# Last expert rows with wide products and separate cross terms, splits two rows ahead, and two early rows placed before the turned picks

## What is computed

```python
q = rmsnorm(h) @ w_q                        # 8 heads
s = q_half @ sub_keys                       # 128 scores for each half of each head
top16 of each half, top16 of their sums     # 16 picks per head and token, weights by softmax
out = sum over picked experts e of  weight[t, e] * gelu(x[t] . u[e]) * v[e]
h = h + out;  return rmsnorm(h, final_norm_g)
```

## Time and profile before

| | |
|---|---|
| median of 3 runs | 1586.64 us (1583.40, 1586.64, 1588.95) |
| profiled execution | 1584.84 us, its span 1583.0 us |
| PE busy | 96% of the span |
| DVE, ACT, POOL busy | 74%, 54%, 22% |
| share of the last chain | PE 82%, DVE 13% |

### The profile page before, as it was taken

How to read it: one execution, slowest core, us unless ns; L and a number is a source line. 1 busy time by engine, 2 the same in 40 slices (tenths; PEclk the granted TensorE clock), 3 DMA queues, 4 the chain that set the end, 5 groups by cost and what they waited for, 6 DMA issues and landing times.

```text
span 1583.0 us, 32051 instructions
## 1 busy us (share of the span) xinstructions
PE 1526.1 (96%) x10720; PEld 1379.4 (87%) x10720; DVE 1178.0 (74%) x2312; ACT 851.2 (54%) x1573; POOL 354.2 (22%) x265
## 2 busy tenths in 40 slices
PE   9899998999999899899999899999999999999997
PEld 7788987999887786698999899988888899999996
DVE  5778676798848678455499778789999777777776
ACT  5564454666548654565455465554444555444455
POOL 3234332011100331222068765630000000000000
PEclk9889999999999999999999999999999999999999
DMA  8323244555565720254656555467777656655654
GB/s 287 119 94 120 81 139 154 153 186 184 187 187 173 253 76 1 80 187 147 194 161 217 183 176 156 152 199 240 242 240 241 210 187 186 185 185 185 187 185 158
DMA packets 89289, 272.22 MB, mean 172 GB/s; under 512 B 9984, under 2 KB 27520, under 8 KB 88832
## 3 DMA queue, kind: packets, MB, share of 16 engines
q1 hardware_dynamic: 65520, 238.06, 47.1%
q10 hardware_dynamic: 23696, 33.17, 6.6%
HBM read 259.13 MB, written 12.06 MB: 171 GB/s over the span
## 4 chain that ended last, share of the span: by engine, by line
PE 82%; DVE 13%; ACT 2%; issue 2%; DMA 1%; POOL 0%; DVEq 0%; ACTq 0%; SPq 0%
PE ps_chunk L508 22%; PE ps_misc L2966 22%; PE ps_chunk L514 11%; PE ps_misc L300 6%; PE ps_chunk L1931 4%; PE ps_chunk L501 3%; PE ps_chunk L520 3%; PE ps_misc L2901 3%; PE ps_chunk L300 2%; PE ps_chunk L524 2%; PE ps_chunk L529 1%; PE ps_misc L1010 1%; DVE mixers_arena L2680 1%; DVE mixers_arena L2679 1%; DVE mixers_arena L2676 1%
## 5 line engine op out<-in xcount | busy, mean ns | idle before, releaser
L425 ACT ACTIVATE w_hi<-raw 128x512 fp32r<-128x512 f32 (+2 forms) x898 | 546.6, 627 | 489.1 <-PE ps_chunk L514 193.7
L432 DVE TENSOR_TENSOR w_lo<-raw,w_hi 128x512 fp32r<-128x512 f32 x663 | 488.6, 755 | 247.1 <-ACT w_hi L425 238.0
L508 PE MATMUL ps_chunk<-x_hi,w_hi 128*128 128x256 f32 x1792 | 459.0, 288 | 2.0 <-ACT w_hi L425 1.6
L508 PE MATMUL ps_chunk<-x_lo,w_hi 128*128 128x256 f32 x1792 | 452.3, 285 | 0.0
L432 POOL TENSOR_TENSOR w_lo<-raw,w_hi 128x512 fp32r<-128x512 f32 (+2 forms) x237 | 311.3, 1329 | 518.8 <-ACT w_hi L425 454.8
L508 PEld LDWEIGHTS ps_chunk<-x_hi,w_hi 128*128 128x128 f32 x1792 | 345.8, 193 | 6.2 <-ACT w_hi L425 2.2
L508 PEld LDWEIGHTS ps_chunk<-x_lo,w_hi 128*128 128x128 f32 x1792 | 346.6, 193 | 2.9 <-issue 0.5
L514 PE MATMUL ps_chunk<-x_hi,w_lo 128*128 128x256 f32 x1792 | 290.0, 285 | 1.9 <-DVE w_lo L432 0.9
L514 PEld LDWEIGHTS ps_chunk<-x_hi,w_lo 128*128 128x128 f32 x1792 | 248.4, 193 | 3.2 <-POOL w_lo L432 2.0
L2966 PE MATMUL ps_misc<-w_hi,hid_hi 128*128 128x512 f32 x508 | 198.3, 390 | 1.6 <-issue 1.6
L2966 PE MATMUL ps_misc<-w_hi,hid_lo 128*128 128x512 f32 x508 | 198.8, 391 | 0.0
(11 more groups left out here) (423 smaller groups left out, 1818.3 us busy)
## 6 DMA issues: line engine op xcount, KB each, us to landing
raw<-in_stream SPq DMA_DIRECT2D x452, 512.0 KB, 3.7
early_rows<-row ACTq DMA_DIRECT2D x68, 128.0 KB, 2.3
row<-early_rows ACTq DMA_DIRECT2D x66, 128.0 KB, 3.1
memory_kv<-mixers_arena ACTq DMA_DIRECT2D x4, 512.0 KB, 5.0
mixers_arena<-in_cmp_w ACTq DMA_DIRECT2D x1, 2048.0 KB, 10.2
mixers_arena<-memory_kv ACTq DMA_DIRECT2D x4, 512.0 KB, 6.4
mixers_arena<-in_consts ACTq DMA_DIRECT2D x1, 1729.0 KB, 10.8
row<-in_rows ACTq DMA_DIRECT2D x3, 512.0 KB, 7.6
```

The source lines that it names most:

```text
L425: e.activation(w_hi[q % 2][:, s], raw[q][:, s], ACT.Copy).then_inc(made, 1)
L432: e.tensor_tensor(w_lo[q % 2][:, s], raw[q][:, s], w_hi[q % 2][:, s].bitcast(F32), ALU.subtract).then_inc(made, 1)
L508: e.matmul(o, w[0][:, k * P:(k + 1) * P], x[:, k, :], start=k == 0 and x is x_hi, stop=False, skip_group_check=True)
```

## The change

1. `x_hi` and `x_lo` become two parts of one tensor `x_both`, so that one matmul of 512 columns can multiply one w_hi tile with both.
2. In the token-major projections, the first half unit of a chunk (q = 0, part = 0) uses the form `run` in place of `by_weights`.
3. `ahead` splits unit q+2 before the gelu of row q (it was q+1), in the selection and the gates stage. The first early v row that had its high split at the head of the next stage has it made already.
4. Of the 36 early rows, 34 stand before the transposes of the picks and 2 behind them.
5. The last 60 rows are rewritten. In PE's queue a row is: 8 wide products (w_hi with x_both, 512 columns), the v row of j-2, 8 narrow ones (w_lo with x_hi, 256 columns). u units always use slot 0, v units slot 1, and the filler units are not split. The wide product leaves w_hi·x_lo in a bank's second 256 columns, so ACT copies them out (`cross_out`), DVE adds the two parts (`summed`), and the gelu runs in place on the sum. ACT's order: cross_out(j-1), gelu(j-1), u highs (j+1), v highs (j-1). DVE's: first half of u lows (j), summed(j-1), second half of u lows, gate_row(j-1), v lows (j-1).

The core of the diff:

```diff
-        x_hi, x_lo = sb("x_hi", [P, KD, T], F32R), sb("x_lo", [P, KD, T], F32R)
+        x_both = sb("x_both", [P, 2, KD, T], F32R)
+        x_hi, x_lo = x_both[:, 0, :, :], x_both[:, 1, :, :]
...
-                        if q == 0 and part == 0 and n:
-                            e.wait_ge(*left[t])
...
-            pe.quiet(by_tiles if not token_major else run if x_made or by_token else by_weights)
+            pe.quiet(by_tiles if not token_major else run if x_made or by_token or (q == 0 and part == 0) else by_weights)
...
-        def ahead(e, q, chunk, i):
-
-            split_hi(e, (q + 1) % 4, chunk + (chunk_early + (q + 1) // 4))
+        def ahead(e, q, chunk):
+
+            split_hi(e, (q + 2) % 4, chunk + (chunk_early + (q + 2) // 4))
...
                 if last:
-                    four(EARLY_SELECT // 4 - 1)
+                    some(EARLY_SELECT // 4 - 1, range(2, UNITS))
                     return
-                four(0)
+                some(0)
                 with e.Fori(1, EARLY_SELECT // 4 - 1) as c:
-                    four(c)
+                    some(c)
+                some(EARLY_SELECT // 4 - 1, range(2))
...
+                def wide_products(b, j):
+                    if later(j, 2):
+                        e.wait_ge(s_summed, j - 1)
+                    else:
+                        e.wait_ge(s_gel, EARLY)
+                    for half in range(2):
+                        e.wait_ge(u_high[half], j + 1)
+                        for k in range(4 * half, 4 * half + 4):
+                            last = e.matmul(ps_chunk[b][:, 0:2 * T], w_hi[0][:, k * P:(k + 1) * P], x_both[:, :, k, :],
+                                            start=k == 0, stop=False, skip_group_check=True)
+                        last.then_inc(u_wide[half], 1)
+
+                def narrow_products(b, j):
+                    for half in range(2):
+                        e.wait_ge(low_made[half], j * 2 + (u0 + 1))
+                        for k in range(4 * half, 4 * half + 4):
+                            last = e.matmul(ps_chunk[b][:, 0:T], w_lo[0][:, k * P:(k + 1) * P], x_hi[:, k, :],
+                                            start=False, stop=k == KD - 1, skip_group_check=True)
+                        last.then_inc(u_done[half], 1)
...
+                for j in range(2):
+                    wide_products(j, j)
+                    narrow_products(j, j)
                 with e.Fori(1, rest // 2) as m:
                     for b in range(2):
-                        u_row(b, m * 2 + b)
-                        v_row(1 - b, m * 2 + (b - 1))
-                unused(e, u0 + 2 * rest)
-                v_last(e, 1, 1, P - 1, u0 + 2 * rest + 1)
+                        wide_products(b, m * 2 + b)
+                        v_row(b, m * 2 + (b - 2))
+                        narrow_products(b, m * 2 + b)
+                v_row(0, rest - 2)
+                v_last(e, 1, 1, P - 1)
...
+                def u_highs(j, q, n):
+                    e.wait_ge(s_w[q], n * 16 + 16)
+                    for half in range(2):
+                        if later(j, 1):
+                            e.wait_ge(u_wide[half], j)
+                            e.wait_ge(low_made[half], j * 2 + (u0 - 1))
...
+                def cross_out(b, j):
+                    e.wait_ge(s_u_done, j + 1)
+                    if later(j, 2):
+                        e.wait_ge(s_summed, j - 1)
+                    e.activation(cross[b], ps_chunk[b][:, T:2 * T], ACT.Copy).then_inc(s_cross, 1)
...
+                def row(b, j, q, n, nn):
+                    cross_out(1 - b, j - 1)
+                    gelu(1 - b, j - 1)
+                    u_highs(j + 1, (q + 2) % 4, nn)
+                    v_highs(j - 1, q + 1, n)
...
+                def row(b, j, q):
+                    u_lows(j, q, (0,))
+                    summed(1 - b, j - 1)
+                    u_lows(j, q, (1,))
+                    gated(1 - b, j - 1)
+                    v_lows(j - 1, q + 1)
```

More of the change, by code:

```diff
@@ L2814, in tensor_rows, with some @@
             def tensor_rows(e, last):
-                def four(c):
-                    for q in range(UNITS):
+                def some(c, rows=range(UNITS)):
+                    for q in rows:
                         bank_left(e, c * 4 + q)
@@ L2829, in four @@
                     for q in range(UNITS):
-                        ahead(e, q, c, None)
+                        ahead(e, q, c)
                         early_gelu(e, q, c * 4 + q)
+                if begin == 0:
+                    split_hi(e, 1, chunk_early)
                 four(begin // 4)
@@ L2986, in times @@
                                     weights[w][:, half * CW:(half + 1) * CW], start=False, stop=stop, skip_group_check=True)
-                for half, high, low, used_up in ((0, s_hi1, s_lo1, s_use1), (1, s_hi, s_lo, s_use)):
+                for half, high, low, used_up in ((0, s_v_high1, s_lo1, s_v_done1), (1, s_v_high, s_lo, s_v_done)):
                     e.wait_ge(s_hih, i + 1)
-                    e.wait_ge(high, u + 1)
+                    e.wait_ge(high, rest)
                     for t in range(TT):
@@ L2995, in v_last @@
                         times(t, half, hid_lo, w_hi)
-                    e.wait_ge(low, u + 1)
+                    e.wait_ge(low, u0 + 2 * rest + 2)
                     for t in range(TT):
@@ L3027, in four @@
                         if not (begin and q == 0):
-                            split_hi(e, q, c + v_chunk)
+                            if not (begin and q == 1):
+                                split_hi(e, q, c + v_chunk)
                             if not (end and q):
@@ L3057, in vector_early @@
                     four(c)
[L3060 to L3064, removed]
-            def tensor_rest(e):
[L3067 to L3070, removed]
-                def v_row(b, j):
[L3073 to L3078, removed]
+            s_u_high1, s_u_high, s_v_high1, s_v_high = (sem(n) for n in ("s_u_high1", "s_u_high", "s_v_high1", "s_v_high"))
@@ new lines, in peer_experts, with later @@
+            halves = [slice(half * CW, (half + 1) * CW) for half in range(2)]
+            def later(j, back):
+                return not isinstance(j, int) or j >= back
+            def tensor_rest(e):
+                def wide_products(b, j):
[16 more added lines that the diff above has]
+                        last.then_inc(u_done[half], 1)
+                def v_row(b, j):
+                    e.wait_ge(s_hid, j + (EARLY + 1))
+                    for half in range(2):
+                        e.wait_ge(low_made[half], j * 2 + (u0 + 4))
+                        for t in range(TT):
+                            last = product3(e, ps_misc[:, 2 * t + half, :],
+                                            [x[:, b, t * P:(t + 1) * P] for x in (hid_hi, hid_lo)],
+                                            [a[1][:, halves[half]] for a in (w_hi, w_lo)], False, False)
+                        last.then_inc(v_done[half], 1)
+                for j in range(2):
+                    wide_products(j, j)
+                    narrow_products(j, j)
@@ new lines, in vector_rest, with u_lows, v_lows, unused @@
+            def vector_rest(e):
+                def u_lows(j, q, some=(0, 1)):
+                    for half in some:
+                        e.wait_ge(u_high[half], j + 1)
+                        if later(j, 1):
+                            e.wait_ge(u_done[half], j)
+                        e.tensor_tensor(w_lo[0][:, halves[half]], raw[q][:, halves[half]],
+                                        w_hi[0][:, halves[half]].bitcast(F32), ALU.subtract).then_inc(low_made[half], 1)
+                def v_lows(j, q):
+                    for half in range(2):
+                        e.wait_ge(v_high[half], j + 1)
+                        e.tensor_tensor(w_lo[1][:, halves[half]], raw[q][:, halves[half]],
+                                        w_hi[1][:, halves[half]].bitcast(F32), ALU.subtract).then_inc(low_made[half], 1)
+                def unused(q, n):
+                    e.wait_ge(s_w[q], n * 16 + 16)
+                    for half in range(2):
+                        e.wait_ge(low_made[half], n * UNITS + q)
+                        e.sem_inc(low_made[half], 1)
+                def summed(b, j):
+                    e.wait_ge(s_u_done, j + 1)
+                    e.wait_ge(s_cross, j + 1)
+                    e.wait_ge(s_own, EARLY + j - 1 if isinstance(j, int) and j > 1 else EARLY if isinstance(j, int) else
+                              j + (EARLY - 1))
+                    e.tensor_tensor(gel[b], ps_chunk[b][:, 0:T], cross[b], ALU.add).then_inc(s_summed, 1)
+                def gated(b, j):
+                    e.wait_ge(s_gel, j + (EARLY + 1))
+                    gate_row(e, b, b, j + EARLY)
+                def row(b, j, q):
[4 more added lines that the diff above has]
+                    v_lows(j - 1, q + 1)
+                u_lows(0, 0)
```

(14 more changed lines are left out.)

48 lines of the change are left out of this document (39 added, 9 removed).

## The result

Seven runs of the changed kernel have a median of 1568.59 us (1566.76 to 1571.87), seven of the kernel before 1583.79 (1577.22 to 1589.71): ratio 0.9897, 95% interval 0.9873 to 0.9922, 15 us less. The same kernel timed again later gave 0.9893 (0.9869 to 0.9918). The profiled execution took 1570.06 us, its span 1568.2, against 1584.84 and 1583.0: 14.8 us less, where 12.0 were forecast.

What follows compares the result with a forecast made beforehand. PE, busy for 96% of the span, was taken as the bound, with DVE setting the selection's end. Gains of 6.9 us in front and 5.1 in the last rows, 12.0 together, gave 1573 us, range 1567 to 1581.

Steps and rivals of the forecast that it cites:

- Two rows moved: Before the picks' transposes: two more early rows fill PE's 5.16 us idle and keep the clock; gates start 6.9 us earlier.
- Splits ahead: Selection and gates: splitting two rows ahead wins nothing, PE's gain disappearing into DVE's end; 0 us, bounds -1 and +1.
- The rule against the change: At the picks: DVE and GpSimd lock shared ports, so POOL's extra work may delay picks; 0 taken, 0.6 us kept.
- Wide products: Last 60 rows: eight 512-column products replace sixteen narrow, saving 0.077 us a row, 4.6 us; bounds 0 and 5.6.
- The smaller estimate beside mine: Last rows: by a fixed cost of about 2.5 ns per matmul, 20 ns a row, 1.2 us in all, time 1576.
- What the new order hides: Last rows: DVE's 4.6 us of 5.53 and ACT's 3.3 fit, slacks all over 1.5 us, PE should never wait.
- Ends of the stage: Last rows' ends: two PE waits for its own last product go, 0.8 us gained; 0.3 us lost at the tail.
- The helper: Token-major projections: PE starts tile 0 sooner but waits for the low part first; 0 us, bounds -0.2 and +1.
- more gain than counted (boundaries, waits in the selection): Stage boundaries and selection waits: more gain than the forecast counted, time about 1567 us; chance 0.04.
- the wide product as dear as two narrow ones: Last rows: a wide product costs what two narrow ones do, gain only 0.5 us, time 1578; chance 0.11.
- the front's gain taken back: Gates stage: waits for POOL, ACT or DVE after the new order lose the 6.9 us, time 1580; chance 0.07.
- DVE as the bound: Last rows: DVE's waits stay beside 4.6 us of work, a row takes 6.16 us, time 1611; chance 0.08.

Runs made afterwards that it cites:

- The run with narrow products: Changed kernel with each 512-column wide product of the last 60 rows replaced by two of 256 columns, order kept; row period 5.62 us against 5.51.
- one row in front: Changed kernel with one of the four early rows before the picks' transposes and three behind; gates' first product at 115.5 us from the anchor, changed kernel 111.0.
- four rows in front: Changed kernel with all four early rows before the picks' transposes, none behind; early v rows begin at 253.7 us from the anchor, changed kernel 249.2.

## Why the prediction was right, step by step

- **Two rows moved: right.** 6.9 us forecast, 6.95 with this part alone. PE was to reach the transposes 0.58 us later than before; alone it does so 0.44 later. The transposes were to take 1.15 us and take 1.28. Behind them two rows (5.74) are enough for DVE's first operands; none is not, by 1.99 us.
- **Splits ahead: the step that failed on its own terms.** I wrote that what PE gains ahead of the picks disappears into DVE's end, and set 0. But by my own sum, with two rows moved, PE arrives 0.7 us behind the picks, so its waits in the selection are on the path. With both parts PE arrives at 104.2 in place of 105.0, and the gates begin another 0.8 us earlier (111.0 for 111.8). A further 0.5 us is won where the early v rows begin (PE's idle time there is 1.03 us, before 1.55). Together they are 1.3 us, more than the bound of 1 that I set for all of it.
- **The rule against the change held, and stayed covered.** The picks come 2.1 us later with the moved rows' work on POOL (104.0) than with POOL out of work (101.9). By the Trainium skill, "SBUF — State Buffer", section "SBUF: two separate sides", a DVE instruction with two SBUF inputs and a GpSimd one that reads SBUF exclude each other on the ports that they share; the 0.43 and 1.48 us of one such sum agree. I had bounded this at one half low part, 1.3 us, over the kernel before, where it was already nearly all paid; that is why nothing was lost.
- **Wide products: right in mechanism, mis-sized.** Forecast 0.077 us a row, measured 0.107. The term that was off is the v row. 0.229 us was the mean of twelve products of which the first run behind narrow ones, and the extra 0.03 us comes once, where 512 columns follow 256. I charged it to the wide products and left it in the v row too, and so counted it twice in the new row; the run with narrow products shows 2.75 there and 1.92 in the high ones. 60 × 0.03 = 1.8 us. The whole gain, 60 × 0.107 = 6.4 us, lies above the bound of 5.6. The smaller estimate beside mine, 20 ns a row and a time of 1576, is not borne out.
- **What the new order hides: right.** PE is busy in all of the 326 us of the stage, with no wait for a sum, a high or a low. The sum takes 0.42 (I took 0.5), cross_out 0.385 (0.364). DVE is busy 0.77 of the stage (0.83 forecast).
- **Ends of the stage: under-counted.** The two drains went, 0.8 us of idle time. The 0.3 us lost at the tail did not come: v_last follows V(58) with no gap (1554.15 + 2.75 = 1556.90, its own start). From the first product of the last rows to the residual it is 337.25 us before and 329.68 after, 7.6 us less where 5.1 were forecast: 1.8 from the v rows, 0.3 from the tail, and 0.4 because what follows a drain is slow as well, which the sum left out. The chain of the kernel before, behind its two drains, then v_last in the changed kernel:

```profile
1239.41 1.19 PE ps_chunk L508 x8
...
1571.63 1.64 PE ps_misc L2985 x6
```
```profile
1556.90 1.48 PE ps_misc L2987 x6
```

Eight products take 1.19 us there and 0.95 elsewhere, six of v_last 1.64 and now 1.48. The run with narrow products, whose rows are as long as before, bears it out: its stage is 1.1 us shorter, near the 0.8 + 0.4 of the drains.
- **The helper: right as far as can be told**, 0 in the whole, a loss at one place.

The sum is 7.8 + 0.5 + 7.6 = 15.9 us behind the anchor, 3.9 more than the 12.0 forecast, and +1.0 ahead of it, which is scatter and hides a part of the miss. That the forecast's own bounds, 1568 to 1577, held is in part luck: the second timing of the same kernel gave 1567.41. The case "more gain than counted (boundaries, waits in the selection)", with a chance of 0.04, is what happened in kind, with the v row's share beside it. Of the rivals, the wide product as dear as two narrow ones, the front's gain taken back and DVE as the bound did not happen; the last needs more than 0.7 us of further DVE work a row, and at 1.4 it is there.

## What to carry to other kernels

When an edit removes the wait that hid another engine's delays, price those delays anew: they were worth nothing while the wait was there and count in full once it is gone. Before charging a rate read from a mixed stream, see whether its excess comes once at a change of shape or with every instruction. Work moved in front of a wait pays until the next stage's operands lose their cover. Here one row less or two more cost over half of the front's gain, about two thirds of that through waiting and one third through the clock. Before comparing medians of a few runs, look at the granted clock that each run lists: here a difference of 0.0017 went with 2 us.

## What the hardware showed beyond the forecast

- TensorE's granted clock over 898 to 900 is 0.52, about the lower level, behind a pause of PE of 5.16 us (kernel before), 0.50 behind one of 3.68 (splits alone) and 0.50 behind one of 2.81 (one row in front); with no pause it is 1.00. Behind waits of 1.99 and 0.89 us with 0.83 us of work between them (four rows in front) it is 0.50 over 908 to 910.
- DVE's cast of 128x512 to bf16 (line 2752) takes 0.43 us with POOL idle and 1.37 to 1.41 beside POOL's half low parts of 1.3 to 1.4 us; a sum of 128x256 (line 2754) takes 0.43 and 1.39 to 1.48.
- For fp32r products with a weight load each, 256 columns take 0.119 us and 512 columns 0.227, so eight matmuls saved are worth 8 × (2 × 0.119 - 0.227) = 0.09 us. A stretch of 512 columns behind one of 256 takes 0.03 us more, once: it is in the row of either kernel. Two runs of 256 columns as one moving operand cost no more than one run of 512.
